# Transposes of a unit and their copy moved ahead of the weighing and high part of the unit before it, in the sparse attention of a two-block network

## What is computed

```
def nsa_attention(q, gates, kc, vc, ks, vs, kw, vw, rel_tbl):
    ...
            s = jnp.einsum('qghd,gnd->ghqn', qf, kc_f) * scale + t5_bias(tq[:, None] - cmp_end[None, :], rel_tbl)
            p_cmp = masked_softmax(s, cmp_end[None, :] <= tq[:, None])
            o_cmp = jnp.einsum('ghqn,gnd->qghd', p_cmp, vc_f)
            ...
            s = jnp.einsum('qghd,gqkd->ghqk', qf, k_sel.astype(jnp.float32)) * scale + t5_bias(dist, rel_tbl)
            p = masked_softmax(s, (dist >= 0)[:, None])
            o_sel = jnp.einsum('ghqk,gqkd->qghd', p, v_sel.astype(jnp.float32))
            ...
            s = jnp.einsum('qghd,gkd->ghqk', qf, k_win) * scale + t5_bias(dist, rel_tbl)
            p = masked_softmax(s, mask)
            o_win = jnp.einsum('ghqk,gkd->qghd', p, v_win)
            gt = jax.nn.sigmoid(gate_c.astype(jnp.float32))
            return gt[..., 0:1] * o_cmp + gt[..., 1:2] * o_sel + gt[..., 2:3] * o_win
```

## Time and profile before

| | |
|---|---|
| median of 3 runs | 2670.41 us (2666.82 to 2671.0) |
| profiled execution, its own time | 2672.61 us |
| span in the trace of that execution | 2670.8 us |
| PE busy | 2447.8 us (92%) |
| DVE busy | 1710.4 us (64%) |
| ACT busy | 1124.5 us (42%) |
| sparse attention, first scores to the last `out_low` | 710.5 to 797.8 us of the span |

### The profile page before, as it was taken

How to read it: one execution, slowest core, us unless ns; L and a number is a source line. 1 busy time by engine, 2 the same in 40 slices (tenths; PEclk the granted TensorE clock), 3 DMA queues, 4 the chain that set the end, 5 groups by cost and what they waited for, 6 DMA issues and landing times. The chain is left out here.

```text
span 2670.8 us, 47235 instructions
## 1 busy us (share of the span) xinstructions
PE 2447.8 (92%) x19417; PEld 2351.2 (88%) x19417; DVE 1710.4 (64%) x2539; ACT 1124.5 (42%) x1594; POOL 103.6 (4%) x139
## 2 busy tenths in 40 slices
PE   7878599997986899979998999999999989999998
PEld 6877499997865899979998889899999988898998
DVE  5664277775463577757775575677777665656776
ACT  4734243333452433333334654433433346544332
POOL 1030000000000000000003000000000030000000
PEclk9889699998897899989999999999999999999999
DMA  8411055555701455525536223454455362234542
GB/s 213 127 64 33 19 195 180 176 177 129 175 17 51 158 179 176 175 86 188 188 127 178 95 95 122 163 180 155 154 174 189 126 178 95 95 127 158 189 160 77
DMA packets 295127, 370.30 MB, mean 139 GB/s; under 512 B 15337, under 2 KB 263778, under 8 KB 294946
## 3 DMA queue, kind: packets, MB, share of 16 engines
q1 hardware_dynamic: 289728, 354.91, 40.6%
q0 software_dynamic: 4880, 13.13, 2.9%
q10 hardware_dynamic: 370, 0.11, 0.0%
HBM read 360.26 MB, written 7.86 MB: 138 GB/s over the span
## 5 line engine op out<-in xcount | busy, mean ns | idle before, releaser
L301 PE MATMUL psum_banks<-source_high,weights_high 128*128 128x272 f32 (+1 forms) x3680 | 1084.2, 295 | 71.5 <-DVE weights_low L1537 23.5
L302 PE MATMUL psum_banks<-source_low,weights_high 128*128 128x272 f32 (+1 forms) x3680 | 1068.5, 290 | 0.0
L303 PE MATMUL psum_banks<-source_high,weights_low 128*128 128x272 f32 (+1 forms) x3680 | 1068.3, 290 | 0.0
L301 PEld LDWEIGHTS psum_banks<-source_high,weights_high 128*128 128x128 f32 x3680 | 714.3, 194 | 83.6 <-DVE weights_low L1537 26.4
L302 PEld LDWEIGHTS psum_banks<-source_low,weights_high 128*128 128x128 f32 x3680 | 714.7, 194 | 0.7
L303 PEld LDWEIGHTS psum_banks<-source_high,weights_low 128*128 128x128 f32 x3680 | 713.5, 194 | 0.0
L1537 DVE TENSOR_TENSOR weights_low<-weight_ring,weights_high 128x2048 fp32r<-128x2048 f32 x102 | 234.8, 2303 | 180.0 <-ACT weights_high L1530 179.3
L301 PE MATMUL psum_banks<-hidden_high,weights_high 128*128 128x272 f32 (+1 forms) x1216 | 349.8, 288 | 0.0
L303 PE MATMUL psum_banks<-hidden_high,weights_low 128*128 128x272 f32 (+1 forms) x1216 | 348.5, 287 | 0.0
L302 PE MATMUL psum_banks<-hidden_low,weights_high 128*128 128x272 f32 (+1 forms) x1216 | 347.3, 286 | 0.0
L1012 DVE TENSOR_TENSOR weights_low<-weight_ring,weights_high 128x2048 fp32r<-128x2048 f32 x131 | 292.8, 2287 | 74.1 <-ACT weights_high L1006 73.9
(11 more groups left out here) (416 smaller groups left out, 2828.6 us busy)
## 6 DMA issues: line engine op xcount, KB each, us to landing
weight_ring<-ffn_w_in SPq DMA_DIRECT2D x88, 1024.0 KB, 6.5
weight_ring<-w_in SPq DMA_DIRECT2D x48, 1024.0 KB, 5.2
weight_ring<-ffn_w_out SPq DMA_DIRECT2D x44, 1024.0 KB, 4.9
weight_ring<-moe_w_gate SPq DMA_DIRECT2D x32, 1024.0 KB, 6.1
weight_ring<-moe_w_up SPq DMA_DIRECT2D x32, 1024.0 KB, 7.2
weight_ring<-moe_w_down SPq DMA_DIRECT2D x32, 1024.0 KB, 4.9
weight_ring<-gdn_w_in SPq DMA_DIRECT2D x16, 1024.0 KB, 5.8
weight_ring<-w_branch SPq DMA_DIRECT2D x12, 1024.0 KB, 5.0
```

What stands on the lines that cost most here:

```text
L301: pe.matmul(out, w_hi, x_hi, start=start, stop=False)
L302: pe.matmul(out, w_hi, x_lo, start=False, stop=False)
L303: return pe.matmul(out, w_lo, x_hi, start=False, stop=stop)
```

## The change

In both loops the step of the unit in hand goes ahead of the step of the unit before it. Operations, waits, buffers and DVE's loop stay as they are. The last step, behind the loops, stays too.

```
                     for t in NSA_FILL.get(u, []):
                         gemm(t)
+                    turn(u)
                     if u:
                         weigh(u - 1)
-                    turn(u)
                 weigh(n_units - 1)
...
                     for t in NSA_FILL.get(u, []):
                         evict(t)
+                    turned_out(u)
                     if u:
                         out_high(u - 1)
-                    turned_out(u)
                 out_high(n_units - 1)
```

## The result

The changed kernel takes 2693.5 us in the median of 4 runs (2693.3 to 2693.8), beside 2670.7 us for the kernel before in the same comparison: 22.8 us more, a ratio of 1.0087 (95% interval 1.0070 to 1.0105). The forecast was 2689.5, in a range of 2680 to 2697. The profiled execution took 2693.35 us.

What follows compares the result with a forecast made beforehand. The prediction took DVE as nearly the bound, with PE waiting. 13.5 us of order plus 5.5 of clock made 19 us on the median of 2670.41, forecast as 2689.5 us, range 2680 to 2697.

Steps and rivals of the forecast that it cites:

- The cover that is taken away: On PE, weigh(13) fills the wait for normalise(14), 769.60 to 771.75 us; the change takes that cover away.
- The copy ahead of the high part: On ACT, the copy now also delays out_low: 0.92 us in three steps, 0.5 in two, 3.8 in all.
- The way through DVE's queue: On DVE, a late out_low(u - 1) delays normalise(u + 1), then turn(u + 1); nearly any delay passes on whole.
- the walk: Both orders followed through all 20 attention steps with the trace's durations; the new order came out 13.5 us slower.
- The seven terms: Delays of out_low at the seven reordered steps, in order: 0, 1.1, 3.7, 0.3, 3.4, 1.2 and 3.8 us.
- Step 4: Projection tiles stand here; out_low(3) comes about 1 us later, hidden by DVE's 1.52 us wait for scores: 0.
- step 6: A last wide unit with a narrow one behind it; out_low, at 745.95 us before, was to come 1.1 us later.
- step 8: A last narrow unit with a wide one behind it; out_low at 755.95 us against 752.25, 3.7 later.
- The clock: TensorE's clock falls behind PE's new waits: three or four more falls at 1.4 to 1.7 us, 5.5; at most some 10.
- a faster kernel: Rival: weighings stop waiting for the copy and the low clock at the end goes, 4.1 us gained, 2666.3; chance 0.04.
- no change: Rival: fills and DVE's waits absorb the delays, the stretch ends within 5 us, about 2670 to 2675; chance 0.05.
- only PE's part counts: Rival: the copy does not hold up the high part and the clock stays up, 9.7 us, 2680; chance 0.14.

Runs made afterwards that it cites:

- pe_only: The kernel before with PE's order alone changed, transposes ahead of the weighing; ACT's order kept: 2691.0 us, ratio 1.0084.
- act_only: The kernel before with ACT's order alone changed, copy of u ahead of the high part of u - 1; PE's order kept: 2684.1 us, ratio 1.0060.
- both_low_later: The changed kernel with out_low(u - 1) moved behind normalise(u + 1) on DVE: 2684.9 us, ratio 1.0058 against the kernel before.
- wide_steps: Both loops of the changed kernel, new order kept in steps 4, 8, 14 and 18 alone: 2693.2 us, ratio 1.0084 against the kernel before.
- narrow_steps: Both loops of the changed kernel, new order kept in steps 6, 10 and 16 alone: 2673.1 us, ratio 1.0008 against the kernel before.

## Why the prediction was right, and where it was off

*The cover that is taken away.* Right. The weighing filled the wait for `normalise`; ahead of the weighing, the transposes wait for it: 19.1 us in eleven times in 740 to 820, where it was 6.2 in seven. `pe_only` shows that this half alone is enough for most of the loss.

*The copy ahead of the high part.* Right in kind. `act_only` shows it alone, 14.5 us. On top of PE's exchange it adds 1.4 us of time (22.8 against 21.4) or 4.9 of stretch (110.4 against 105.4), around the 3.8 that the prediction gave the copies.

*The way through DVE's queue.* It is the one that bounds the changed kernel, as the `out_low` rows show, but it does not carry most of the loss: with `out_low` out of the way the change still costs 18.8 of 22.8 us. The second way, from the weighing over ACT's copy to the next transposes, is in the trace of `both_low_later`, and the prediction does not name it. How what remains there splits was not tried. By the walk behind the two expectations 6.9 us of it are order (4.6 more than before against 2.3 less); that would leave some 10 of the 17.0 of stretch to the clock, an estimate.

*The seven terms.* With the clock held up they measured 1.4, 3.8, 0.3, 3.5, 1.3 and 3.9, a sum of 14.2, taken with 37 additions in PE's queue, where the prediction had 1.1, 3.7, 0.3, 3.4, 1.2 and 3.8, a sum of 13.5. Step 4 was hidden as it said: in `wide_steps`, where step 4 is in the new order and step 6 in the old, `out_low(3)` comes 1.5 us later than before and `out_low(5)` does not, and DVE's wait of 1.52 us before the scores is gone. `narrow_steps` has 1.3, 0.3 and 1.3 at its three places; 1.6 more appears at step 8, which is in the old order there, behind a clock of 0.80 and 0.64 in 749 to 755.

*The clock.* This is the term that was mis-sized. I took 5.5 us, three or four falls more at 1.4 to 1.7; the stretch gained about 10, 24.2 less 14.2, the upper bound that I had given. The falls were five against one before, four more, so that the count was right and the price of one was not: about 2.5 us. Windows of 1 us show the clock low in 747 to 755, 757 to 765, 771 to 782, 798 to 806 and 808 to 816. Counting the windows at the edges by their share, that is about 7 us for four of them and 10 for the third, and not the 3 to 4 of the one in the earlier trace rows. A turn with most or all of a weighing fell into four of them. The waits themselves came out as walked (2.44, 2.80, 3.27 and 3.45 us before the turns of 9, 15, 18 and 19, where the prediction had 2.5, 2.8, 3.4 and 3.5), but not which of them a fall would meet: one fall came at the start of the wait of 1.72 us before `turn(8)`, 2.2 us behind one of 1.42, and one at `turn(12)`, while during and after the wait before `turn(15)` the clock stood at 1.00:

```profile
785.00:786.00 1.00, 0.00 (x0) 0.00 (x0) 0.97 (x2) 0.83 (x5) 0.00 (x0) 1.00 0.08 16
```

```profile
786.36 1.09 PE L2280 MATMUL psum_banks<-consts_common,scores 128*128 128x128 f32 x8 [2.80 <-DVE scores L2503]
```

The Trainium skill's rule ("TensorE: Matmul & The Clock Gate", on HAM oscillation) is that work behind idle periods starts at the half rate. The trace agrees at the turns of 8, 9, 18 and 19, which took 1.97 us each, and not at `turn(15)`, which took 1.09; there the measurement decides. What picks the waits that a fall meets stays open; the length of the wait alone does not.

*The sum.* 19 us forecast, 24.2 of stretch measured: the clock's term is 4.5 larger and the steps' 0.7. The time, 22.8, is 1.4 less than the stretch grew, so it lies nearer to the forecast than the terms do. The top of the range was not added up: 13.5 and at most 10 of clock are 23.5, not 26. The rivals of a faster kernel and of no change are out, and so is the one in which only PE's part counts with the clock up, 9.7 us, since `pe_only` alone lost 21.4. As for the faster one, the weighings' waits for the copy did shrink, by 4.4 us with weight loads and matmuls added together, and it bought nothing, since the transposes' waits, counted alike, grew by 27.

## What to carry to other kernels

Before moving a step forward in an engine's queue, look whether its input is ready at the new place: a block that ran "without idle time" in front of it may have been the very thing that hid the wait. When the queue of another engine is nearly full, follow what stands behind the late result there; here moving that result's consumer behind the next useful step gained 3.5 us in the old order, where both exchanges on PE and ACT lost. In the new order it did not take the loss away, since the next transposes then waited for the copy: look for the second way too before counting on it. And price the waits on TensorE twice, once as time and once as a clock that falls behind them, over the whole burst that follows.

## What I had not expected of the hardware

A float32 matmul of 256 columns stands in the trace as two records and cost 0.45 us of PE in a row of 20 (4.58 us), so additions planned by the record came out twice too long. Idle time filled with work that nobody reads made the changed kernel faster: with the clock at 1.00 the changed kernel's stretch shrank by 11.5 us. And the clock fell at waits of 1.4 and 1.7 us at one place and stayed up through one of 2.8 at another, so in this kernel the length of a single wait did not decide it.
